# A two-model kernel on one core: RWKV's preparation moved into latent attention's block, behind retention, with scores from one matmul and values added at every step

## The reference

```python
z_a, z_b, z_c = split_cols(h @ w_in[l], [RWKV_COLS, MLA_COLS, RET_COLS])
o_a = rwkv7_mixer(z_a, ...)      # 4 heads of 64, forward and backward
o_b = mla_mixer(z_b, ...)        # latent attention, 8 heads
o_c = retention_mixer(z_c, ...)
x = x + g2 * (concatenate([o_a, o_b, o_c]) @ w_out[l])
```

```python
q = ((rms_norm(cq) * q_norm_g) @ w_uq).reshape(B, S, H, 64 + 32)
kv = ((rms_norm(ckv) * kv_norm_g) @ w_ukv).reshape(B, S, H, 64 + 64)
s = einsum('bqhd,bkhd->bhqk', q_nope, k_nope) + einsum('bqhr,bkr->bhqk', q_pe, k_pe)
o = softmax(s * (96 ** -0.5)) @ v
```

## Time and profile before

| | before |
|---|---|
| median of 3 runs | 3824.22 us (3815.29 to 3830.31) |
| the profiled execution's own time | 3824.96 us |
| its span, first to last instruction | 3823.2 us |
| PE busy | 3555.1 us, 93% of the span |
| DVE busy | 1800.7 us, 47% |
| ACT busy | 1201.7 us, 31% |
| POOL busy | 623.8 us, 16% |
| mean granted clock of PE | 0.973 |

### The profile page before, as it was taken

How to read it: one execution, slowest core, us unless ns; L and a number is a source line. 1 busy time by engine, 2 the same in 40 slices (tenths; PEclk the granted TensorE clock), 3 DMA queues, 4 the chain that set the end, 5 groups by cost and what they waited for, 6 DMA issues and landing times. The chain is left out here.

```text
span 3823.2 us, 51724 instructions
## 1 busy us (share of the span) xinstructions
PE 3555.1 (93%) x21980; PEld 2780.5 (73%) x21980; DVE 1800.7 (47%) x2526; ACT 1201.7 (31%) x1651; POOL 623.8 (16%) x424
## 2 busy tenths in 40 slices
PE   7999999597999999999977899999889999989999
PEld 6888783285888788877437678876668887757887
DVE  5666534645444556653365433334444334254332
ACT  3222324423222322233352332224433223343223
POOL 4202000231202120210014111210002121001112
PEclk9999999898999999999998999999999999989999
DMA  6565320002443356442000233322023332112331
GB/s 194 176 195 164 113 68 24 5 4 90 125 145 115 111 164 189 147 128 79 24 5 3 79 88 94 95 88 80 23 78 100 99 99 81 56 55 88 99 99 56
DMA packets 443674, 355.88 MB, mean 93 GB/s; under 512 B 15478, under 2 KB 440500, under 8 KB 443444
## 3 DMA queue, kind: packets, MB, share of 16 engines
q1 hardware_dynamic: 443444, 352.57, 29.3%
HBM read 350.43 MB, written 2.10 MB: 92 GB/s over the span
## 5 line engine op out<-in xcount | busy, mean ns | idle before, releaser
L570 DVE TENSOR_TENSOR ring_wlo<-ring_raw,ring_whi 128x2048 fp32r<-128x2048 f32 (+4 forms) x270 | 576.7, 2136 | 406.3 <-ACT ring_whi L551 374.1
L551 ACT ACTIVATE ring_whi<-ring_raw 128x2048 fp32r<-128x2048 f32 (+3 forms) x278 | 491.2, 1767 | 534.3 <-PE f_ps L860 255.5
L858 PE MATMUL f_ps<-act_hi,ring_whi 128*128 128x512 f32 x1280 | 502.5, 393 | 3.3 <-DVEq L989 3.3
L860 PE MATMUL f_ps<-act_hi,ring_wlo 128*128 128x512 f32 x1280 | 498.6, 390 | 0.0
L859 PE MATMUL f_ps<-act_lo,ring_whi 128*128 128x512 f32 x1280 | 498.2, 389 | 0.0
L948 POOL TENSOR_TENSOR f_glo<-f_v,f_ghi 128x512 fp32r<-128x512 f32 x88 | 237.5, 2699 | 1084.6 <-ACT f_ghi L940 1084.6
L858 PEld LDWEIGHTS f_ps<-act_hi,ring_whi 128*128 128x128 f32 x1280 | 240.4, 188 | 53.8 <-DVEq L989 5.0
L860 PEld LDWEIGHTS f_ps<-act_hi,ring_wlo 128*128 128x128 f32 x1280 | 240.3, 188 | 51.1
L858 PE MATMUL f_ps<-f_ghi,ring_whi 128*128 128x512 f32 x704 | 277.4, 394 | 0.0
L859 PEld LDWEIGHTS f_ps<-act_lo,ring_whi 128*128 128x128 f32 x1280 | 240.5, 188 | 49.0
L933 ACT ACTIVATE f_t<-f_ps 128x512 f32<-128x512 f32 x88 | 52.6, 598 | 710.2 <-PE f_ps L860 656.3
(11 more groups left out here) (520 smaller groups left out, 6101.1 us busy)
## 6 DMA issues: line engine op xcount, KB each, us to landing
ring_raw<-in_w_ff_in SPq DMA_DIRECT2D x176, 512.0 KB, 4.8
f_ada_raw<-in_w_ada SPq DMA_DIRECT2D x128, 512.0 KB, 5.4
ring_raw<-in_w_mlp SPq DMA_DIRECT2D x64, 1024.0 KB, 5.2
ring_raw<-in_w_in SPq DMA_DIRECT2D x42, 1024.0 KB, 5.1
ring_raw<-in_w_ff_out SPq DMA_DIRECT2D x32, 768.0 KB, 4.5
ring_raw<-in_w_ff_out SPq DMA_DIRECT2D x32, 640.0 KB, 4.1
ring_raw<-in_w_out SPq DMA_DIRECT2D x16, 1024.0 KB, 5.5
ada_raw<-in_w_ada SPq DMA_DIRECT2D x16, 512.0 KB, 7.8
```

Of the source, the lines that this page charges most:

```text
L551: eng.activation(self.w_hi[:, i % self.SPLIT, 0:s.nk, 0:w], self.raw[:, i % self.RAW, 0:s.nk, 0:w], ACT.Copy)\
L570: eng.tensor_tensor(self.w_lo[:, i % self.SPLIT, 0:s.nk, 0:w], self.raw[:, i % self.RAW, 0:s.nk, 0:w], self.w_hi[:, i % self.SPLIT, 0:s.nk ...
L858: eng.matmul(out, wh, o_hi[:, a, :], start=(s.first and q == 0), stop=False)
L860: mm = eng.matmul(out, wl, o_hi[:, a, :], start=False, stop=(s.last and q == s.nk - 1))
```

## The change

`mixers_1` now runs `project_shifted`, `retention`, a new stage `attention_and_features`, `rwkv_chunks` and `rwkv_states`. The function `rwkv` is gone: its first block's work is written into the instruction lists of latent attention's stage. Three things change in how attention itself is done. Keys and queries get a tile for each head, in which the 64 `nope` rows and the 32 rotary rows stand in one piece, so that `scores` is one matmul for each head; for even heads these are rows 0 to 95, for odd heads rows 0 to 127, of which POOL sets rows 0 to 31 to zero. The rotary rows get there by 16 transfers within the core's memory on SP's queue. The values are taken one step at a time, over the 128 query tokens of that step. The class `Early` lays the projection's tensors, attention's weights and RWKV's features over one another in one tensor of 16 x 512 columns. The semaphore sets grow from 44 to 60.

```diff
+def attention_and_features(nc, k, ph, l, z_rw, early, ups, vt, small, gate, o):
...
+            eng.wait_ge(key_done, 1)
+            for h in range(H):
+                r = rope_rows(h % 2)
+                eng.dma_start(keys[r, h, :], kr[r, :]).then_inc(key_put, 16)
+            for g in (0, 1):
+                eng.wait_ge(q_ready, g + 1)
+                for e in range(4):
+                    eng.dma_start(queries[rope_rows(e % 2), 4 * g + e, :], qr[rows(e, 32), g, :])\
+                       .then_inc((query_put0, query_put1)[g], 16)
...
+            for i in range(4):
+                lora(i)
+            norm_sums((0, 1), ps[6])
+            lora(4)
+            lora(5)
+            norm_sums((2, 3, 4), ps[7])
+            lora(6)
+            lora(7)
...
                 for e in (0, 1):
-                    eng.matmul(ps[2 * (n % 2) + e][:, :], qn[rows(e), p, i * P:(i + 1) * P], kn[rows(e), p, :],
-                               start=True, stop=False)
-                for e in (0, 1):
-                    r = rows((2 * p + e) % 4, 32)
-                    eng.matmul(ps[2 * (n % 2) + e][:, :], qr[r, p // 2, i * P:(i + 1) * P], kr[r, :], start=False, stop=True)\
-                       .then_inc(scored, 1)
+                    h = 2 * p + e
+                    r = head_rows(h)
+                    eng.matmul(ps[2 * (n % 2) + e][:, :], queries[r, h, i * P:(i + 1) * P], keys[r, h, :],
+                               start=True, stop=True).then_inc(scored, 1)
...
+            def values(n):
+                p, i = n // 4, n % 4
+                eng.wait_ge(p_copied, 2 * n + 2)
+                if i == 0 and p >= 2:
+                    eng.wait_ge(o_copied, p - 1)
+                for j in range(4):
+                    for e in (0, 1):
+                        h = 2 * p + e
+                        mm = eng.matmul(ps[6 + p % 2][rows(e), i * P:(i + 1) * P], v[:, j, h * MLA_V:(h + 1) * MLA_V],
+                                        pt[:, n % 2, e, j, :], start=(j == 0), stop=(j == 3))
+                mm.then_inc(valued, 1)
+
+            for n in range(STEPS + 3):
                 if n < STEPS:
                     scores(n)
                 if 2 <= n < STEPS + 2:
                     turn(n - 2)
-                if n >= 6:
-                    values((n - 6) // 4, (n - 6) % 4)
+                if n >= 3:
+                    values(n - 3)
...
+                if n in (1, 5, 9):
+                    powers((n + 3) // 4)
...
+            odd = [t[:, :, :].rearrange("p (q e) s -> p q e s", e=2)[0:32, :, 1, :] for t in (keys, queries)]
+            for t in odd:
+                eng.memset(t, 0.0).then_inc(zeroed, 1)
...
+                if n % 4 == 0:
+                    eng.wait_ge(e_done, 3 * c + 3)
+                    ins = eng.tensor_tensor(chunks(feat["A"][:, c, :]), chunks(kk[:, t, :]), exclusive(Ep, c), ALU.mult)
...
+                if n < STEPS:
+                    feature(n)
+                if n >= 8 and n % 4 == 0:
+                    put_out(n // 4 - 2)
+            put_out(3)
```

## The result

The changed kernel takes 3755.68 us (median of 4 runs, 3753.36 to 3761.37), the kernel before 3823.8 beside it. The ratio is 0.9821, with a 95% interval from 0.9803 to 0.984: faster by 68 us. The forecast was 3751, with a range from 3733 to 3785.

What follows compares the result with a forecast made beforehand. PE bounds attention, not the preparation, which can hide beside it. Joined stage: front 49.5, loop 64.3, boundary 0.3, 114.1 us for 150.2; with chunks -1, -37.1 a layer, -74.2 from 3824.96: 3751 us (range 3733 to 3785).

Steps and rivals of the forecast that it cites:

- The two bounds: PE bounds attention's front and loop but not the preparation, whose DVE, ACT and POOL work fits beside attention's loop.
- The front: Attention's start up to the first scores: 39.59 us before, 49.54 with the preparation's PE work added.
- The step: One steady step of attention's loop: 3.81 us instead of 4.14, with PE still the bound.
- the lower bound for the values: In a loop step, eight value calls over 128 columns cost pure column work, 1.01 us; upper bound 1.76.
- POOL: POOL's six operations falling into attention's loop stretch DVE's work beside them: +2 us a layer.
- The tail: Attention's loop end: a chain of 6.7 us behind the last scores, which take 1.78.
- Retention is the same in either place: Retention, moved ahead of attention, takes the same time and stays out of the sum: 0 us.
- The forecast's clock rows: Profile rows with PE's clock at 0.50 after 3.21 us idle, 1.00 after 1.65; used to price stage starts.
- The chunks: RWKV's chunks stage, no longer begun at a low PE clock after 27.71 us idle: -1 us a layer (0 to -2).
- rival 2: Attention's front stalls on 16 serial transfers at 2.6 us each, or a late DVE operation: 3758 to 3766; chance 0.18.
- DVE was not the bound: Against a rival where attention's loop becomes DVE's (3763) or the values chain badly (3775); chance 0.20.
- Rival 4: Repeated PE waits of some 3 us in the joined stage keep PE at 1.2 GHz: 3855 us; chance 0.02.

Runs made afterwards that it cites:

- the repeat: The changed kernel run again unedited, beside the other trials on the same chip: 3757.02 us, ratio 0.9816.
- both overload trials: Changed kernel with one more feature-sized DVE product behind each of 16 features a layer: 3766.25 us; changed kernel with 16 rotary transfers a layer cut into 64: 3771.88 us.

## Why the prediction was right, point by point

- **The two bounds** were read rightly. PE was the bound in attention and not in the preparation, and the preparation's work found room beside it. Attention's own edits alone gave 11 us of 68; the larger part is the hiding.
- **The front** was 50.36 for 49.54: the first pairs cost what their half-clock row said (3.71 for 3.55), and the half clock reached into the square sums (2.82 us, where layer 1 and a warm start have 1.98).
- **The step** was 3.82 for 3.81, with both of its new prices (1.83 for two score calls, 1.03 for the values). Taking the lower bound for the values was right.
- **POOL** was oversized: 2 us a layer, measured 0.5. The mechanism held, the size didn't: I carried over 9 us of POOL time from a stage in which its operations took 0.94 to 2.16 us each, and in the loop they took 0.77 to 1.27. The Trainium skill's rule quoted ahead (GPSIMD Engine Reference, Key points) would have the scalings stretch as well; they did, 1.78 for 0.88, but in one step a layer only, so its 3 us were further off.
- **The tail** was undersized: from the last scores on 729.39 - 718.55 = 10.84 us, with 729.39 the end of DVE's copy of the last output, for the 1.78 + 6.7 = 8.48 of the forecast. I added up the chain of step 15 alone and forgot that PE has the turnings of steps 13 and 14 and the values of steps 12 to 14 to do then, and that ACT's list puts the copies behind the exponentials. Turning the copies forward gave 1.1 to 1.3 us. Its error and POOL's partly cancel: the loop took 65.4 us for 64.3.
- **"Retention is the same in either place"** is the step that failed: +1.7 and +3.0 us. The experiments show that moving it is enough (+2.8, +2.9), and that it is PE's clock (matmuls in the idle time take it back in full). They also show 1.6 to 2.1 us more in retention's old place, in three of four layers behind a changed loop, so even leaving it where it stood might not have kept its time. The forecast's clock rows were applied to two stage starts and not to retention, whose own waits of 3 us stood in the same trace.
- **The chunks** at -1 was right in size, by the first 10 us.
- **The rivals.** The transfers were hidden (2.7 us to spare, for 3.2 in the forecast, which had four issued in 1.7 us where they take 2.5). With four times as many the front stalls as rival 2 said, but by the count of issues: one was issued every 0.63 to 0.67 us and landed 1.8 us later, so they did not go one behind the other. DVE was not the bound, with 0.55 us to spare, and becomes it with one more operation a step, at the price that slack predicts. Rival 4, the half clock, did occur, and its scale in retention was 1.7 to 3.0 us a layer and not 52.

Summed over both layers with the measured sizes: retention +4.7 for 0, the stage -69.2 for -72.2, the chunks -2.8 for -2, the states -0.1 and the rest of the program -4.2 for 0, in all -71.6 for -74.2. The first two are misses of 7.7 us, which the runs explain; the other 5 us that came back are of the size by which the repeat moved with no edit, and I don't claim a cause for them. That the profiled execution came within 2.4 us of the forecast is therefore partly luck: 5 us that nobody forecast hide most of 7.7 us of misses. The medians, 4.7 us above the forecast, are the fairer measure.

## What to carry to other kernels

Where a stage bound by PE stands next to one that is not, add up each engine's work over the joined instruction lists; here that gave the joined stage within 2 us a layer, and the slack read from one step gave both overload trials within 1 us a layer, as long as only waits are counted. Then ask where PE becomes idle, as for 3.2 and 3.3 us here, since a stage that is only moved can get another clock behind the same wait; a few matmuls without use in such gaps, with one reordering on ACT, took 9.8 us from the stages here, on top of the 68. Read a term of 1 us from rows at a fixed place, not from totals of a stage.

## What the runs showed of the hardware

- PE's clock isn't a function of the code. One retention stage ran at a mean of 0.85 in layer 0 and 0.93 in layer 1 of the same execution, behind the same first wait of 3.18 us, and took 36.2 and 34.1 us. In the changed kernel the clock stayed at 1.00 behind a wait of 3.27 us in layer 0 (the next matmuls took 1.99) and fell only behind the next wait, of 3.10; in layer 1 it fell behind the 3.27 (2.79).
- A wait can cost more than its length: with 5.35 us of waiting for transfers the stage in layer 0 became 7.3 us longer.
- 64 transfers of 16 KB inside the core's memory take SP 0.63 to 0.67 us each, 16 of 64 KB 0.63 us, and land 1.8 and 2.0 us later (medians), so that several are under way at once; I had bounded them by a load's 2.6 us each, one behind the other. The Trainium skill's rule quoted with rival 2 (DMA: Bandwidth & Descriptors, Rules for kernel authors), that such transfers serialise, is not borne out here in the sense of rival 2: none waited for the one ahead to land.
- A DVE operation on 128 x 2 elements took 1.00 us instead of 0.17 beside one of POOL's, so a small operation can be held up as long as a large one.
